# Attention values as the loaded operand in column halves, and softmax inverses applied afterwards to x

## The chip, the cores and the metric

The kernel runs on one core of a Trainium2 chip. The metric is the device time of one launch in microseconds; three runs of the kernel before gave 2671.84, 2673.00 and 2675.21 us, median 2673.0. The core has a matrix engine (TensorE, PE in the profile; its weight loads are a row of their own, PEld), VectorE (DVE), ScalarE (ACT), GpSimdE (POOL) and SyncE (SP), which here only issues DMAs. Each engine runs its own instructions in order and waits on semaphores that the others count up.

## The reference

Two layers of a hybrid block on 1024 tokens with 1024 features, fp32. Cut to the attention, which is what the change touches:

```
h = rms_norm(x); proj = h @ w_in             # q|k|v of mixer A, q|k|v of mixer B, two gates
A (8 heads of 64): per 64-token chunk, keys of the own chunk and 8 chunks before
   sc = q k^T / 8 + bias(relative distance);  p = softmax(sc);  y_a = (p v) @ w_branch_a
B (8 query heads, 2 key heads): rotary q, k; keys of 2 chunks
   m = max(max(sc), sink);  p = exp(sc - m) / (sum exp(sc - m) + exp(sink - m))
   y_b = (p v) @ w_branch_b
x = x + (sigmoid(gate_a) * y_a + sigmoid(gate_b) * y_b) @ w_out
x = x + SwiGLU(rms_norm(x));  after the last layer: rms_norm(x)
```

## The kernel before, in words

Activations lie feature-major (128 partitions are features, the free dimension is tokens). Most matmuls split fp32 numbers into a high and a low part (three matmuls each, `three` at L1191 to L1196 and `product` at L1203 to L1205). The attention of a layer is a hand-written pipeline over 128 units. Four groups g of 32 units follow each other; the first 16 units of a group are mixer A, the last 16 mixer B. A unit is one head and one block of queries: u is even for the first head of a pair (e = 0) and odd for the second (e = 1), and two neighbouring units share the block p. An A unit has 128 queries and nb = min(p + 1, 5) blocks of 128 keys, a B unit 2 times 64 queries (rows of both) and one block of 128 keys. So over the eight p of a group nb is 1, 2, 3, 4, 5, 5, 5, 5.

Every engine has its own loop `for s in range(UNITS + ...)`, and step s of each does the part that has come so far:
- PE: `scores(s)` (L1337, L1338), one gate step (three matmuls of 512 columns, L1191 to L1196), `turn(s - 2)` (L1348: transposes of the probabilities into PSUM tile `t_ps`), `weigh(s - 3)` (L1373), more gate steps, and each second step `turn_pair` (L1383). Gate steps are the fill: the tables `FILL_A` and `FILL_B` say how many stand in which step. Now and then `turn_values` (L1312) transposes two blocks of values.
- DVE: `row_max(s)` (L2603) adds the bias and takes the maximum of the scores; `invert_pair` (L2622) takes the reciprocals of two units; `take_heads` (L2632) multiplies the output of a pair by them on the way out of PSUM into `o_tok`. It also splits staged queries and keys and applies the rotary factors.
- ACT: `soften(s)` (L1741, the exponential with its row sum), `take_turned(s - 2)` (L1753, copies the turned probabilities from PSUM to `probs_t`), `take_pair` (L1764, L1767, copies the turned pair into `x_sb`), and copies of staged queries, keys and values.
- SP issues loads and stores: staged blocks, weight tiles, gate logits.

What the change starts from, in three lines: the turned probabilities are the loaded operand (128 columns) and 64 columns of values stream; the result has tokens on its partitions, so a pair of heads is scaled there and turned back by PE.

```
mm = pe.matmul(o_ps(u)[:, e * HD:(e + 1) * HD], probs_t[u % 2][:, j * P:(j + 1) * P], values[j], ...)   # L1373
dve.tensor_tensor(o_tok ..., o_ps(u) ..., inverse, ALU.mult)                                            # L2632
pe.transpose(p_ps, o_tok[:, n % 2, :], ident[:, :])                                                     # L1383
```

`t_ps`, the score tile of mixer A and the output tile of A are single: a turn waits until ACT has copied the one before it, scores of A until DVE has taken the maximum of the ones before. After the loop PE does `last_gates` (16 gate steps), ACT and DVE split `x_sb` into `o_hi` and `o_lo` (`split_o`, L1799, L2672), and `branches` uses these eight tiles in order.

## Time and profile before

| what | us |
|---|---|
| median of three runs | 2673.0 |
| profiled execution, whole | 2678.14 |
| its span, first to last instruction | 2676.2 |
| PE busy (share of the span) | 2631.9 (98%) |
| PEld, DVE, ACT busy | 2208.2 (83%), 1923.2 (72%), 1159.0 (43%) |

The span is cut by the program into two layers, and each layer into the input projection, the attention, the branches and output projection, and the feed-forward part. The profile has no names for these; they are found by the lines of the instructions. A matmul in fp32 (not split by hand) shows as two PE records, with a weight load each; a matmul of the split parts and a transpose show as one. In the timeline a record's length includes the way through the array, so neighbouring records overlap: what one costs in a full stream is the distance from its start to the next start.

### The profile page before, as it was taken

How to read it: one execution, taken by the hardware profiler on the slowest of the kernel's cores; microseconds unless marked ns; L12 is line 12 of the kernel's file. 1: busy time of each engine (PE TensorE's matmuls, PEld its weight loads, DVE VectorE, ACT ScalarE, POOL GpSimd, SP SyncE). 2: the span in 40 equal slices, each digit the busy share in tenths (PEclk: the TensorE clock that was granted, in tenths of full speed). 3: DMA queues.
4: the chain of work that ended last, by engine and by line, in shares of the span. 5: the costliest groups of instructions: out<-in, count | busy, mean ns of one | idle time of the engine just before them, and what ended most of it. 6: DMA issues, size and time to landing. Idle time of an engine off the chain costs nothing. (4 is left out here: it accounts for less than half of the span.)

```text
span 2676.2 us, 36725 instructions
## 1 busy us (share of the span) xinstructions
PE 2631.9 (98%) x12920; PEld 2208.2 (83%) x12920; DVE 1923.2 (72%) x3579; ACT 1159.0 (43%) x2429; POOL 252.6 (9%) x390
## 2 busy tenths in 40 slices
PE   8999999999999999999999999999999999999998
PEld 6888888888888888888878888888888888888886
DVE  8766667644787787767996666775448887776687
ACT  6222677732533333344542227775325333333444
POOL 0000311244100000000000011112440000000000
PEclk9999999999999999999999999999999999999999
DMA  4323433253222332385423243332531332234843
GB/s 147 122 104 115 155 102 111 75 183 115 87 99 103 114 118 84 106 269 176 153 99 122 99 144 123 119 97 88 188 120 61 114 110 88 103 114 136 267 124 126
DMA packets 185236, 333.21 MB, mean 125 GB/s; under 512 B 17248, under 2 KB 62688, under 8 KB 185056
## 3 DMA queue, kind: packets, MB, share of 16 engines
q1 hardware_dynamic: 176832, 307.67, 34.6%
q10 hardware_dynamic: 8224, 23.20, 2.6%
q8 instruction: 105, 1.72, 0.3%
q14 instruction: 75, 0.61, 0.1%
HBM read 237.09 MB, written 92.80 MB: 123 GB/s over the span
## 5 line engine op out<-in xcount | busy, mean ns | idle before, releaser
L1203 PE MATMUL ps<-op_hi,up_hi 128*128 128x512 f32 x1232 | 479.9, 390 | 2.5 <-DVE third_sum L2781 2.5
L1205 PE MATMUL ps<-op_hi,up_lo 128*128 128x512 f32 x1232 | 479.3, 389 | 0.0
L1204 PE MATMUL ps<-op_lo,up_hi 128*128 128x512 f32 x1232 | 479.3, 389 | 0.0
L1203 PE MATMUL ps<-in_hi,up_hi 128*128 128x512 f32 x728 | 286.9, 394 | 3.3 <-DVE up_lo L2279 2.1
L1205 PE MATMUL ps<-in_hi,up_lo 128*128 128x512 f32 x728 | 285.0, 392 | 0.0
L1204 PE MATMUL ps<-in_lo,up_hi 128*128 128x512 f32 x728 | 285.0, 392 | 0.0
L1878 ACT ACTIVATE up_hi<-up_raw 128x512 fp32r<-128x512 f32 x252 | 158.0, 630 | 276.9 <-PE ps L1205 271.1
L1203 PEld LDWEIGHTS ps<-op_hi,up_hi 128*128 128x128 f32 x1232 | 231.3, 188 | 51.1 <-issue 3.3
L1205 PEld LDWEIGHTS ps<-op_hi,up_lo 128*128 128x128 f32 x1232 | 231.3, 188 | 48.3
L1204 PEld LDWEIGHTS ps<-op_lo,up_hi 128*128 128x128 f32 x1232 | 231.3, 188 | 47.6
L1173 POOL CAST w_hi<-w_raw 128x256 fp32r<-128x256 f32 x192 | 85.3, 486 | 1757.7 <-DMA w_raw<-w_lin 1199.7
L1203 PE MATMUL ps<-act_hi,dn_hi 128*128 128x512 f32 x616 | 240.5, 390 | 1.4 <-DVE dn_lo L2956 1.4
L1204 PE MATMUL ps<-act_lo,dn_hi 128*128 128x512 f32 x616 | 239.7, 389 | 0.0
L1205 PE MATMUL ps<-act_hi,dn_lo 128*128 128x512 f32 x616 | 239.7, 389 | 0.0
L1592 ACT ACTIVATE up_hi<-w_quarter 128x512 fp32r<-128x512 f32 x156 | 96.7, 628 | 192.5 <-PE ps L1205 180.4
L1905 ACT ACTIVATE act_hi<-act_raw 128x512 fp32r<-128x512 f32 x154 | 97.0, 630 | 176.1 <-DMA act_raw<-ff_saved 173.3
L2748 DVE TENSOR_TENSOR up_lo<-up_raw,up_hi 128x512 fp32r<-128x512 f32 x252 | 172.7, 687 | 0.0
L1177 POOL TENSOR_TENSOR w_lo<-w_raw,w_hi 128x256 fp32r<-128x256 f32 x192 | 168.6, 907 | 0.0
L1203 PEld LDWEIGHTS ps<-in_hi,up_hi 128*128 128x128 f32 x728 | 138.1, 190 | 33.0 <-DVE up_lo L2279 4.1
L2954 DVE TENSOR_TENSOR act_lo<-act_raw,act_hi 128x512 fp32r<-128x512 f32 x154 | 106.3, 690 | 82.0 <-ACT act_hi L1905 81.3
L1204 PEld LDWEIGHTS ps<-in_lo,up_hi 128*128 128x128 f32 x728 | 138.1, 190 | 28.5
L1205 PEld LDWEIGHTS ps<-in_hi,up_lo 128*128 128x128 f32 x728 | 137.7, 189 | 28.9
(266 smaller groups left out, 5406.8 us busy)
## 6 DMA issues: line engine op xcount, KB each, us to landing
up_raw<-w_gu SPq DMA_DIRECT2D x42, 1024.0 KB, 5.1
act_raw<-ff_saved SPq DMA_DIRECT2D x154, 256.0 KB, 2.7
w_quarter<-w_lin SPq DMA_DIRECT2D x52, 512.0 KB, 4.4
w_raw<-w_lin SPq DMA_DIRECT2D x48, 512.0 KB, 3.7
ff_saved<-ff_block SPq DMA_DIRECT2D x88, 256.0 KB, 2.0
ff_saved<-ff_mix SPq DMA_DIRECT2D x66, 256.0 KB, 2.1
gated<-gates_saved SPq DMA_DIRECT2D x32, 512.0 KB, 4.1
stage<-in_saved SPq DMA_DIRECT2D x48, 256.0 KB, 2.8
```

The costliest lines, as they stand in the source:

```text
L1173: pool.tensor_copy(w_hi[slot][:, k, :], w_raw[raw][:, k, :]).then_inc(hi_made, 1)
L1177: op = pool.tensor_tensor(w_lo[slot][:, k, :], w_raw[raw][:, k, :], w_hi[slot][:, k, :], ALU.subtract)
L1203: pe.matmul(out, w1, x1, start=first, stop=False, skip_group_check=True)
L1204: pe.matmul(out, w1, x0, start=False, stop=False, skip_group_check=True)
L1205: return pe.matmul(out, w0, x1, start=False, stop=last, skip_group_check=True)
L1592: act.activation(up_hi[s % PRODUCTS][:, :, :], in_weight(q, i), ACT.Copy).then_inc(in_raised, 1)
L1878: act.activation(up_hi[s % PRODUCTS][:, :, :], up_src(q, i), ACT.Copy).then_inc(up_raised, 1)
L1905: act.activation(act_hi[r][:, :], act_raw[r][:, :], ACT.Copy).then_inc(act_raised, 1)
L2748: dve.tensor_tensor(up_lo[s % PRODUCTS][:, :, :], up_src(q, i), up_hi[s % PRODUCTS][:, :, :], ALU.subtract).then_inc(up_split, 1)
L2954: dve.tensor_tensor(act_lo[r][:, :], act_raw[r][:, :], act_hi[r][:, :], ALU.subtract)
```

## The change

The operands of `weigh` change places: 64 columns of values are loaded and the 128 turned probabilities stream. The two heads of a pair write partitions 0 to 63 and 64 to 127 of the output, so that each uses half of the array's columns, and the two heads alternate. The result is feature-major and goes unscaled into `x_sb` (DVE copies it from PSUM). `turn_pair`, `o_tok` and `take_pair` go. The reciprocals are taken for eight units at a time, turned by PE as an 8 by 128 block (`turn_inverse`, step 8k + 10 for units 8k to 8k + 7), copied to SBUF by DVE, stored to DRAM by SP (step 8k + 11), loaded back as rows that are repeated over 64 partitions each (steps 8k + 12 and 8k + 16, four units each time) and multiplied into `x_sb` in place by DVE (steps 8k + 15 and 8k + 19). There are three `probs_t` instead of two. In mixer B two units are turned one after the other and copied at once. `weigh` runs once per pair, at even steps. The gate steps keep their number per phase and move between steps (`FILL_A`, and `FILL_B`'s rounding); all logits but the last go through one buffer; `vb_odd` lies in two pieces.

```diff
 NPROBS = 3
-NSTAT = 8
+NTURNED = 3
+ODD_FIRST = 3
+NSTAT = 16
...
-FILL_A = ((3, 3, 3, 2, 2, 2, 2, 1, 1, 1, 1, 1, 1, 1, 1, 1), (1, 1, 1, 1, 1, 0, 1, 0, 1, 0, 0, 0, 1, 0, 0, 0))
+FILL_A = ((3, 3, 3, 3, 2, 3, 1, 2, 1, 1, 0, 1, 1, 1, 0, 1), (1, 1, 0, 1, 0, 1, 0, 1, 0, 1, 0, 1, 0, 1, 0, 0))
...
+TURNED_AT, SAVED_AT, SPREAD_AT, SCALED_AT = 10, 11, (12, 16), (15, 19)
...
-        probs_t = [at(f"probs_t{i}", [P, A_COLS], F32, 101 * KB + 2560 * i) for i in range(2)]
+        probs_t = [at(f"probs_t{i}", [P, A_COLS], F32, (101 * KB, 103 * KB + 512, TAB + 5 * KB + 512)[i]) for i in range(NTURNED)]
...
+        inverse_rows = at("inverse_rows", [P, 2 * P], F32, TAB + 14592)
...
+            def save_inverse(L, eight):
+
+                n = L * EIGHTS + eight
+                sp.wait_ge(inverse_step, 2 * n + 2)
+                sp.dma_start(inverse_dram[n], inverse_turned[0:EIGHT, :]).then_inc(inverse_saved, 16)
+
+            def spread_inverse(L, quarter):
+
+                n = L * QUARTERS + quarter
+                sp.wait_ge(inverse_saved, 16 * (n // 2 + 1))
+                if n > 0:
+                    sp.wait_ge(head_scaled, n)
+                for e in range(2):
+                    src = inverse_dram[n // 2][QUARTER * (n % 2):QUARTER * (n % 2 + 1), :].rearrange("(p e) n -> e p n", e=2)
+                    sp.dma_start(inverse_rows[e * HD:(e + 1) * HD, :].rearrange("d (p n) -> d p n", p=2),
+                                 src[e:e + 1].to_broadcast([HD, 2, P])).then_inc(inverse_spread, 16)
...
-                for s in range(UNITS + 3):
+                for s in range(UNITS + SPREAD_AT[1]):
+                    if eight_at(s, SAVED_AT) is not None:
+                        save_inverse(L, eight_at(s, SAVED_AT))
+                    for quarter in quarters_at(s, SPREAD_AT):
+                        spread_inverse(L, quarter)
...
-                    pe.wait_ge(turned_ready, L * UNITS + u)
+                if u > 0 and (mixer == "A" or e == 0):
+                    pe.wait_ge(turned_ready, L * TURN_GROUPS + groups_turned(u - 1))
...
+                first = e if mixer == "B" else 0
                 for j in range(key_blocks(mixer, p)):
-                    mm = pe.transpose(t_ps[:, j * P:(j + 1) * P], probs[u % NPROBS][:, j * P:(j + 1) * P], ident[:, :])
+                    mm = pe.transpose(t_ps[:, (first + j) * P:(first + j + 1) * P], soft(u)[:, j * P:(j + 1) * P], ident[:, :])
                 mm.then_inc(turned, 1)
...
             def weigh(L, u):
 
...
                 nb = key_blocks(mixer, p)
+                n = L * HEAD_PAIRS + u // 2
                 if mixer == "A":
...
+                    blocks = [va[:, p + 1 - nb + j, :] for j in range(nb)]
+                    turns = [turned_to(u - 1), turned_to(u)]
...
                 else:
...
+                    blocks = [vb[:, chunk // 2, :] if chunk % 2 or chunk == 0 else odd_values(chunk // 2 - 1)]
+                    turns = [turned_to(u)[:, e * P:(e + 1) * P] for e in range(2)]
...
-                pe.wait_ge(turned_ready, L * UNITS + u + 1)
-                n = L * (UNITS // 2) + u // 2
...
+                pe.wait_ge(turned_ready, L * TURN_GROUPS + groups_turned(u))
                 taken = n - 1 if mixer == "B" and u % PHASE > 1 else n
-                if e == 0 and taken > 0:
+                if taken > 0:
                     pe.wait_ge(head_free, taken)
                 for j in range(nb):
-                    mm = pe.matmul(o_ps(u)[:, e * HD:(e + 1) * HD], probs_t[u % 2][:, j * P:(j + 1) * P], values[j],
-                                   start=(j == 0), stop=(j == nb - 1))
+                    for e in range(2):
+                        rows = slice(e * HD, (e + 1) * HD)
+                        mm = pe.matmul(o_ps(u)[rows, :], blocks[j][:, rows], turns[e][:, j * P:(j + 1) * P],
+                                       start=(j == 0), stop=(j == nb - 1))
                 mm.then_inc(head_done, 1)
 
-            def turn_pair(L, u):
-
-                n = L * (UNITS // 2) + u // 2
-                pe.wait_ge(head_free, n + 1)
-                if n > 0:
-                    pe.wait_ge(pair_ready, n)
-                pe.transpose(p_ps, o_tok[:, n % 2, :], ident[:, :]).then_inc(pair_turned, 1)
+            def turn_inverse(L, s, eight):
+
+                pe.wait_ge(inverse_step, 2 * (L * EIGHTS + eight) + 1)
+                if values_before(s) > 0:
...
+                pe.transpose(i_ps, inverse[:, stats_of(eight)], ident[:, :]).then_inc(inverse_turned_done, 1)
...
-                for s in range(UNITS + 5):
+                for s in range(UNITS + 3):
+                    steps = fill_steps(s)
+                    if s % PHASE == 0 and s > 0:
+                        for i, k in steps[:1]:
+                            gate_step(L, i, k)
+                        steps = steps[1:]
                     if s < UNITS:
                         scores(L, s)
-                    steps = fill_steps(s)
                     for i, k in steps[:1]:
                         gate_step(L, i, k)
-                    if 2 <= s < UNITS + 2:
-                        turn(L, s - 2)
-                    if 3 <= s < UNITS + 3:
+                    u = s - 2
+                    if 0 <= u < UNITS:
+                        if unit(u)[0] == "A":
+                            turn(L, u)
+                        elif u % 2:
+                            turn(L, u - 1)
+                            turn(L, u)
+                    if eight_at(s, TURNED_AT) is not None:
+                        turn_inverse(L, s, eight_at(s, TURNED_AT))
+                    if s >= 4 and s % 2 == 0:
                         weigh(L, s - 3)
                     for i, k in steps[1:]:
                         gate_step(L, i, k)
-                    if s > 5 and s % 2 == 0:
-                        if values_before(s) > 0:
-                            pe.wait_ge(v_ready, L * VALUES + values_before(s))
-                        turn_pair(L, s - 5)
                     for c, part in turns_at(s):
-                        if s > 6:
-                            pe.wait_ge(pair_ready, L * (UNITS // 2) + (s - 5) // 2)
+                        if inverses_before(s + 1) > 0:
+                            pe.wait_ge(inverse_step, 2 * (L * EIGHTS + inverses_before(s + 1)))
                         turn_values(L, c, part)
...
-                act.activation(probs_t[u % 2][:, 0:cols], t_ps[:, 0:cols], ACT.Copy).then_inc(turned_ready, 1)
...
+                act.activation(turned_to(u)[:, 0:cols], t_ps[:, 0:cols], ACT.Copy).then_inc(turned_ready, 1)
...
             def split_o(L):
-                act.wait_ge(pair_ready, (L + 1) * (UNITS // 2))
+                act.wait_ge(head_free, (L + 1) * HEAD_PAIRS)
+                act.wait_ge(inverse_saved, 16 * (L + 1) * EIGHTS)
                 for j in range(KT):
+                    if j == 0:
+                        act.wait_ge(head_scaled, (L + 1) * QUARTERS - PHASE // QUARTER)
+                    if j == KT - 2:
+                        act.wait_ge(head_scaled, (L + 1) * QUARTERS)
                     if j == XK:
...
+            def take_inverse(L, eight):
+
+                n = L * EIGHTS + eight
+                dve.wait_ge(inverse_turned_done, n + 1)
+                if n > 0:
+                    dve.wait_ge(inverse_saved, 16 * n)
+                dve.tensor_copy(inverse_turned[0:EIGHT, :], i_ps).then_inc(inverse_step, 1)
 
             def take_heads(L, u):
 
-                n = L * (UNITS // 2) + u // 2
-                dve.wait_ge(head_done, L * UNITS + u + 1)
-                dve.wait_ge(inverse_ready, n + 1)
-                if u >= 4:
-                    dve.wait_ge(pair_turned, n - 1)
-                inverse = stat[:, u % NSTAT - 1:u % NSTAT + 1, 6:7].to_broadcast([P, 2, HD])
-                dve.tensor_tensor(o_tok[:, n % 2, :].rearrange("p (e d) -> p e d", e=2),
-                                  o_ps(u).rearrange("p (e d) -> p e d", e=2), inverse, ALU.mult).then_inc(head_free, 1)
...
+                n = L * HEAD_PAIRS + u // 2
...
+                dve.wait_ge(head_done, n + 1)
+                src = o_ps(u) if mixer == "A" else o_ps(u).rearrange("p (h n) -> p h n", h=2)
+                dve.tensor_copy(x_of(u), src).then_inc(head_free, 1)
...
+            def scale_heads(L, quarter):
+
+                mixer, g, _, p = unit(QUARTER * quarter)
+                n = L * QUARTERS + quarter
+                dve.wait_ge(head_free, L * HEAD_PAIRS + 2 * quarter + 2)
+                dve.wait_ge(inverse_spread, 32 * (n + 1))
+                if mixer == "A":
+                    x = x_sb[:, g, p * P:(p + 2) * P]
+                    dve.tensor_tensor(x, x, inverse_rows[:, :], ALU.mult).then_inc(head_scaled, 1)
...
-                for s in range(UNITS + 5):
+                for s in range(UNITS + SCALED_AT[1]):
+                    if s < UNITS:
+                        row_max(L, s)
+                    if eight_at(s, TURNED_AT) is not None:
+                        take_inverse(L, eight_at(s, TURNED_AT))
                     if s % 2 == 1 and 5 <= s < UNITS + 4:
                         take_heads(L, s - 4)
-                    if s < UNITS:
-                        row_max(L, s)
-                    if s % 2 == 0 and 1 <= s <= UNITS:
-                        invert_pair(L, s - 1)
+                    for late in range(2):
+                        eight = eight_at(s - late, EIGHT)
+                        if eight is not None:
+                            sunken = unit(EIGHT * eight)[0] == "B"
+                            if late == 0 and sunken:
+                                add_sinks(L, eight)
+                            if late == (1 if sunken else 0):
+                                invert(L, eight)
+                    for quarter in quarters_at(s, SCALED_AT):
+                        scale_heads(L, quarter)
```

Below, L numbers in the rows of the changed kernel are its own: L1440 and L1441 are the scores (L1337 and L1338 before), L1452 the turn (L1348), L1480 `weigh` (L1373), L1489 `turn_inverse`, L1294 to L1299 a gate step (L1191 to L1196), L1415 `turn_values` (L1312).

On PE, first layer, group 0 of mixer A, at the units with two key blocks, the rows before are:

```order
L1348 MATMUL ps<-ident,probs_107 128x128 x3
L1373 MATMUL ps<-va,probs_t_110 128x64 x2
L1191 MATMUL ps<-in_hi_52,w_hi_225 128x512
L1195 MATMUL ps<-in_lo_59,w_hi_225 128x512
L1196 MATMUL ps<-in_hi_52,w_lo_227 128x512
L1383 MATMUL ps<-ident,o_tok 128x128
L1337 MATMUL ps<-ka_hi_92,qs_88 128x512
L1338 MATMUL ps<-ka_lo_94,qs_88 128x512
L1191 MATMUL ps<-in_hi_52,w_hi_225 128x512
L1195 MATMUL ps<-in_lo_59,w_hi_225 128x512
L1196 MATMUL ps<-in_hi_52,w_lo_227 128x512
L1348 MATMUL ps<-ident,probs_108 128x128 x3
```

and with the change, from the same turn on:

```order
L1452 MATMUL ps<-ident,probs_108 128x128 x3
L1480 MATMUL ps<-probs_t_112,va 64x128
L1480 MATMUL ps<-probs_t_110,va 64x128
L1480 MATMUL ps<-probs_t_112,va 64x128
L1480 MATMUL ps<-probs_t_110,va 64x128
L1440 MATMUL ps<-ka_hi_92,qs_88 128x512
L1441 MATMUL ps<-ka_lo_94,qs_88 128x512
L1294 MATMUL ps<-in_hi_52,w_hi_231 128x512
L1298 MATMUL ps<-in_lo_59,w_hi_231 128x512
L1299 MATMUL ps<-in_hi_52,w_lo_233 128x512
L1452 MATMUL ps<-ident,probs_109 128x128 x3
```

The output matmuls of a unit (two rows of one kind before) have become four, alternating between the two heads, all in one step of the pair; the next step has none, and the pair's transpose is gone.

On PE, same group, between two turns of full length (five key blocks), the rows before are:

```order
L1348 MATMUL ps<-ident,probs_106 128x128 x5
L1373 MATMUL ps<-va,probs_t_109 128x64 x5
L1312 MATMUL ps<-ident,stage_103 128x128 x2
L1337 MATMUL ps<-ka_hi_91,qs_87 128x256
L1338 MATMUL ps<-ka_lo_93,qs_87 128x256
L1337 MATMUL ps<-ka_hi_91,qs_87 128x384
L1338 MATMUL ps<-ka_lo_93,qs_87 128x384
L1191 MATMUL ps<-in_hi_50,w_hi_225 128x512
L1195 MATMUL ps<-in_lo_57,w_hi_225 128x512
L1196 MATMUL ps<-in_hi_50,w_lo_227 128x512
L1348 MATMUL ps<-ident,probs_107 128x128 x5
```

and with the change:

```order
L1452 MATMUL ps<-ident,probs_109 128x128 x5
L1415 MATMUL ps<-ident,stage_103 128x128 x2
L1440 MATMUL ps<-ka_hi_91,qs_87 128x256
L1441 MATMUL ps<-ka_lo_93,qs_87 128x256
L1440 MATMUL ps<-ka_hi_91,qs_87 128x384
L1441 MATMUL ps<-ka_lo_93,qs_87 128x384
L1452 MATMUL ps<-ident,probs_107 128x128 x5
L1480 MATMUL ps<-probs_t_111,va 64x128
```

Between these two turns stood the output matmuls of a unit, values, scores and a gate step; now values and scores stand there, and the output matmuls of both units come behind the second turn.

On DVE, first layer, in a phase of mixer B, the rows before are (`o_tok` is the scaled pair):

```order
L2603 ISA probs_106,stat<-ps,b_zeros,less_sinks 128x128
L2603 ISA stat 128x1
L2620 TENSOR_TENSOR stat<-stat 128x2
L2622 RECIPROCAL stat<-stat 128x2
L2551 TENSOR_TENSOR ka_lo_94<-stage_102,ka_hi_92 128x512
L2632 TENSOR_TENSOR o_tok<-ps,stat 128x128
L2603 ISA probs_107,stat<-ps,b_zeros,less_sinks 128x128
L2603 ISA stat 128x1
L2609 TENSOR_TENSOR stat<-sink_rows,stat 128x2
```

and with the change (`inverse_turned` are the turned reciprocals, `inverse_rows` what came back from DRAM):

```order
L2736 TENSOR_TENSOR sink_term<-row_sum,sink_term 128x8
L2738 RECIPROCAL inverse<-sink_term 128x8
L2715 ISA probs_109,neg_max<-ps,b_zeros,less_sinks 128x128
L2715 ISA neg_max 128x1
L2746 COPY inverse_turned<-ps 8x128
L2715 ISA probs_107,neg_max<-ps,b_zeros,less_sinks 128x128
L2715 ISA neg_max 128x1
L2758 COPY x_sb<-ps 128x2x64
L2768 TENSOR_TENSOR x_sb<-x_sb,inverse_rows 128x256
L2715 ISA probs_108,neg_max<-ps,b_zeros,less_sinks 128x128
L2715 ISA neg_max 128x1
```

The multiplication out of PSUM and the two small instructions of each pair are gone; a plain copy, the turned reciprocals and a multiplication in `x_sb` stand there, and the maximum of the next scores (L2715, L2603 before) is queued behind each of them.

## Rows read from the trace of the kernel before

**Rows 1.** The page, part 1: busy time of each engine.

```profile
PE 2631.9 (98%) x12920; PEld 2208.2 (83%) x12920; DVE 1923.2 (72%) x3579; ACT 1159.0 (43%) x2429; POOL 252.6 (9%) x390
```

**Rows 2.** Stretches: the attention of both layers (busy us, granted clock, DMA).

```profile
282.00:530.00 248.00, 240.29 (x1684) 213.98 (x1684) 166.63 (x551) 183.00 (x563) 43.64 (x63) 0.99 0.34 105
1592.00:1840.00 248.00, 241.29 (x1700) 215.64 (x1698) 168.01 (x559) 179.59 (x560) 36.03 (x59) 1.00 0.34 106
```

**Rows 3.** Groups by line on PE, 281 to 533 us: records, busy, mean ns.

```profile
L1373 PE MATMUL ps<-va,probs_t 128*128 128x64 f32 x480 | 60.9, 269 | 1.0 <-DVE o_tok L2632 1.0
...
L1373 PE MATMUL ps<-vb,probs_t 128*128 128x64 f32 x72 | 12.2, 251 | 0.1
...
L1373 PE MATMUL ps<-vb_odd,probs_t 128*128 128x64 f32 x56 | 9.3, 248 | 0.0
```

**Rows 4.** Timeline of PE, mixer A, five key blocks (start us, length us).

```profile
1807.16 1.23 PE L1373 MATMUL ps<-va,probs_t 128*128 128x64 f32 x10
...
1808.26 0.36 PE L1337 MATMUL ps<-ka_hi,qs 128*128 128x256 f32 x1
...
1808.93 0.71 PE L1348 MATMUL ps<-ident,probs 128*128 128x128 f32 x5
1809.48 1.23 PE L1373 MATMUL ps<-va,probs_t 128*128 128x64 f32 x10
...
1811.73 1.23 PE L1373 MATMUL ps<-va,probs_t 128*128 128x64 f32 x10
```

**Rows 5.** Timeline of PE: fp32 records with one streamed column, and with 128.

```profile
2032.29 1.84 PE L1214 MATMUL ps<-ones,sumsq 128*128 128x1 f32 x16
2033.99 0.49 PE L1203 MATMUL ps<-op_hi,up_hi 128*128 128x512 f32 x1
...
2050.45 1.95 PE L1235 MATMUL ps<-ident,rstd_col 128*128 128x128 f32 x16
2052.15 0.48 PE L1203 MATMUL ps<-op_hi,up_hi 128*128 128x512 f32 x1
```

**Rows 6.** Timeline, PE's rows, one unit of mixer B.

```profile
392.39 0.27 PE L1348 MATMUL ps<-ident,probs 128*128 128x128 f32 x1
...
392.95 0.45 PE L1191 MATMUL ps<-in_hi,w_hi 128*128 128x512 f32 x1
...
393.25 0.40 PE L1195 MATMUL ps<-in_lo,w_hi 128*128 128x512 f32 x1
...
393.71 0.27 PE L1348 MATMUL ps<-ident,probs 128*128 128x128 f32 x1
```

**Rows 7.** Groups by line and shape on ACT, 281 to 533 us.

```profile
L1741 ACT ACTIVATE probs<-probs,stat 128x640 f32<-128x640 f32 x32 | 26.4, 826 | 0.4
L1741 ACT ACTIVATION_READ_ACCUMULATOR probs<-probs,stat 128x1 f32 x128 | 24.4, 190 | 0.0
L1753 ACT ACTIVATE probs_t<-ps 128x640 f32<-128x640 f32 x32 | 22.5, 703 | 17.3 <-PE ps L1348 16.7
```

**Rows 8.** Timeline: from a turn through ACT's copy to the next turn.

```profile
1836.78 0.27 PE L1348 MATMUL ps<-ident,probs 128*128 128x128 f32 x1
...
1837.09 0.28 ACT L1753 ACTIVATE probs_t<-ps 128x128 f32<-128x128 f32 x1 [0.49 <-PE ps L1348]
...
1837.51 0.30 PE L1348 MATMUL ps<-ident,probs 128*128 128x128 f32 x1 [0.29 <-ACT probs_t L1753]
```

**Rows 9.** DMA issues, 281 to 533 us: count, KB each, us to landing.

```profile
gates_saved<-logit SPq DMA_DIRECT2D x14, 256.0 KB, 2.1
...
swapped<-in_saved SPq DMA_DIRECT2D x28, 64.0 KB, 2.4
```

**Rows 10.** Timeline, end of the second layer's attention: DVE, and PE's first branch matmul.

```profile
1841.70 5.93 DVE L2672 TENSOR_TENSOR o_lo<-x_sb,o_hi 128x1024 fp32r<-128x1024 f32 x4 [2.00 <-ACT o_hi L1799]
1848.62 4.81 DVE L2672 TENSOR_TENSOR o_lo<-x_sb,o_hi 128x1024 fp32r<-128x1024 f32 x4 [0.98 <-ACT o_hi L1799]
```

**Rows 11.** Timeline of PE, the same place.

```profile
1852.76 0.39 PE L1191 MATMUL ps<-o_hi,w_hi 128*128 128x512 f32 x1
```

More of the change, by code:

```diff
@@ L45 @@
 NPROBS = 3
-NSTAT = 8
+NTURNED = 3
+ODD_FIRST = 3
+NSTAT = 16
+QUARTER = 4
 GROUPS = 4
@@ L264, in unit, with number_b, eight_at, quarters_at @@
     return "AB"[r // PHASE], g, r % 2, r % PHASE // 2
-def number_b(u):
-    g, r = divmod(u, UNITS_PER_GROUP)
-    return g * PHASE + r - PHASE + 1
+def number_b(eight):
+    g, r = divmod(EIGHT * eight, UNITS_PER_GROUP)
+    return (g * PHASE + r - PHASE) // EIGHT
+def eight_at(s, at):
+    return (s - at) // EIGHT if s >= at and (s - at) % EIGHT == 0 and s - at < UNITS else None
+def quarters_at(s, at):
+    return [2 * eight_at(s, a) + j for j, a in enumerate(at) if eight_at(s, a) is not None]
+def own_steps(L, sinks):
+    return L * (1 + 2 * B_EIGHTS) + 1 + sinks
+def inverses_before(s):
+    return sum(eight_at(j, TURNED_AT) is not None for j in range(s))
+def groups_turned(u):
+    g, r = divmod(u + 1, UNITS_PER_GROUP)
+    return g * (PHASE + PHASE // 2) + min(r, PHASE) + max(r - PHASE, 0) // 2
+TURN_GROUPS = GROUPS * (PHASE + PHASE // 2)
+HEAD_PAIRS = UNITS // 2
+QUARTERS = UNITS // QUARTER
+EIGHT = 2 * QUARTER
+EIGHTS = UNITS // EIGHT
+B_EIGHTS = EIGHTS // 2
+TURNED_AT, SAVED_AT, SPREAD_AT, SCALED_AT = 10, 11, (12, 16), (15, 19)
 def raw_slot(t):
@@ L557, in o_ps, with x_of, stat_of, stats_of @@
             return bank(5 if mixer == "B" and u // 2 % 2 else 6)[:, 0:P]
+        def x_of(u):
+            mixer, g, _, p = unit(u)
+            if mixer == "A":
+                return x_sb[:, g, p * P:(p + 1) * P]
+            tile, chunk = GROUPS + g // 2 * 2, chunk_of(g, p)
+            return x_sb[:, tile:tile + 2, chunk * CHUNK:(chunk + 1) * CHUNK]
+        def stat_of(u):
+            return slice(u % NSTAT, u % NSTAT + 1)
+        def stats_of(eight):
+            first = EIGHT * eight % NSTAT
+            return slice(first, first + EIGHT)
+        i_ps = bank(7)[0:EIGHT, 2 * P:3 * P]
+        def turned_to(u):
+            mixer, _, _, _ = unit(u)
+            return probs_t[u % NTURNED if mixer == "A" else u // 2 % 2]
+        def odd_values(block):
+            return vb_odd[0][:, block, :] if block < ODD_FIRST else vb_odd[1][:, block - ODD_FIRST, :]
+        def logit_of(i):
+            return logit[1 if i == GATE_HALVES - 1 else 0][:, :]
+        def soft(u):
+            mixer, _, _, _ = unit(u)
+            first = u // NPROBS % 2 * P if mixer == "B" else 0
+            return probs[u % NPROBS][:, first:first + (P if mixer == "B" else A_COLS)]
+        def soft_last(u):
+            mixer, _, _, _ = unit(u)
+            return u - (2 * NPROBS if mixer == "B" and u % PHASE >= NPROBS else NPROBS)
         v_ps = bank(7)[:, 0:2 * P]
@@ L1738, in soften @@
                 act.wait_ge(scores_free, L * UNITS + u + 2)
[L1739 to L1745 removed]
+                buf = soft(u)
@@ L1782, in attention @@
                         soften(L, s)
+                    if eight_at(s, EIGHT) is not None and unit(s - 1)[0] == "B":
+                        soften_sinks(L, eight_at(s, EIGHT))
                     for e in range(2):
```

168 lines of the change are left out of this document (89 added, 79 removed).

## The prediction

> **What bounds the kernel now.** I read the busy times first, then the stretches of the two attentions, PE's groups by line there, and the timeline of single units. The reader is to see that PE is busy for 98% of the span [rows 1], and for 240 and 241 of the 248 us of each attention at a granted clock of 0.99 to 1.00, its upper level of 2.4 GHz, while ACT is busy for 183 and DVE for 168 us at most [rows 2]. So a us that PE loses in the attention is a us of the kernel, as long as the others can follow. The change touches nothing outside the two attentions and their ends.
>
> What PE's time consists of there: sixteen fp32 records that stream one column each take 1.70 us (2032.29 to 2033.99), and sixteen that stream 128 columns take 1.70 us as well (2050.45 to 2052.15), 0.106 us a record [rows 5]. A record of 64 columns cannot be cheaper, then: what it pays for is the load of 128 columns, not its stream. The output matmuls have 480, 72 and 56 such records in the first layer, 608 [rows 3], so 608 x 0.106 = 64.4 us per layer. The unit of five key blocks shows the whole: 2.32 us from one unit's output matmuls to the next with a pair transpose between, 2.25 without, scores 0.67 (1808.26 to 1808.93), turn 0.55 [rows 4].
>
> **The change part by part, per layer.**
>
> Output matmuls. The same number of matmuls and records is left (two heads times nb blocks times two records for each pair), but each loads 64 columns, streams 128, and the two heads use different halves of the array. I take a record's stream at 0.106, which [rows 5] give as its most, and let the halves overlap: the second record of one head runs beside the first of the other, so a pair takes 2nb + 1 slots of 0.106 instead of 4nb. Mixer A: nb adds up to 30 over eight pairs, 68 slots, times four groups 272; mixer B: 32 pairs of 3 slots, 96. 368 x 0.106 = 39.0 us: a gain of 25.4. If the halves do not overlap it is 608 slots again and the gain is 0; no record of before uses half of the array, so these are the ends.
>
> The Trainium skill ("TensorE: Matmul & The Clock Gate", LDWEIGHTS) says that a weight load costs its columns at 1.2 GHz, whatever the rows; by it 64 columns cost an estimated 53 ns. The one-column rows agree with it at 128 columns (0.106 against its 0.107); no row here loads 64.
>
> Pair transposes. 64 go, at 0.07 each (2.32 less 2.25): 4.5 gained. 16 transposes of reciprocals come, at most the same: 1.1 lost.
>
> Switches between the whole array and its halves. Before, every matmul has the whole array; now PE goes to halves and back for each of 64 pairs, and once more for each of 16 reciprocal blocks: 144 switches per layer. No trace shows one. From below: 0. From above: the next load waits until the record before has left the array, 0.269 mean length [rows 3] less 0.106 = 0.163, and then stands open for 0.106: 0.27. The nearest thing that the trace shows is a load that is not covered: the first 512-column record behind short ones takes 0.30 (392.95 to 393.25) where the next two take 0.23 each (393.25 to 393.71) [rows 6]. I take this 0.07, since a switch at the least uncovers a load: 144 x 0.07 = 10.1 lost.
>
> New wait for the copy. `t_ps` is single. Before, between two turns lay output matmuls and scores; now, from an odd step to the next even one, only scores, and sometimes values or a gate step. The way through ACT: 0.31 from a record's start to the copy's start (1836.78 to 1837.09), 0.14 from the copy's end to the next turn [rows 8], and a copy of 640 columns takes 0.703 [rows 7]. Five records of a turn: 0.44 + 0.31 + 0.70 + 0.14 = 1.59 from its start, against 0.55 + 0.67 = 1.22 without the wait: 0.37. A gate step (three times 0.23) covers it wholly, a pair of values mostly. Behind the first group this leaves, for each group, two units at 0.37, one of four blocks at about 0.26 and some 0.6 for the small ones: 1.6, times three 4.8; the first group has gate steps there. 4.8 lost. Queued behind the waiting turn on PE are the output matmuls of a pair and the next scores, so DVE and ACT wait with it.
>
> Reciprocals through DRAM. DVE wants the rows five steps after it has copied the turned block, then four steps after that. A small store lands after 2.1 and a small load after 2.4 us [rows 9]: 4.5, with handoffs about 5, against five units of mixer B at 1.32 (392.39 to 393.71, [rows 6]), 6.6. It fits, so I put it at 0; behind a late row DVE's next maximum would be queued, and PE's scores behind that. SP stands still for these landings too, and stage loads queue behind it; 2 us of that lie within the steps that these loads are ahead.
>
> End of the attention. The last four pairs' rows need the store and two loads one behind the other, 6.9 us, before `split_o` may take the last tiles; on DVE the whole of `o_lo` stands behind that multiplication. Before, `o_lo` runs from 1841.70 to 1853.43 [rows 10] and PE wants the eight tiles from 1852.76 on [rows 11], one per 0.69 (three records of 0.23, [rows 6]), the last at 1857.6. About 6 us later (the pair's transpose and copies drop out of the way) `o_lo` would end at 1859.4, 1.8 late: 1.8 lost.
>
> DVE and ACT. DVE's maximum and ACT's exponential stay; 64 multiplications out of PSUM become copies, 64 pairs of reciprocals become 16 blocks, 32 multiplications of 256 columns come; ACT loses the pair copies and half of B's turn copies. Both get lighter and have room [rows 2]: 0. The gate steps keep their number: 0. The logit store lands within 2.1 us [rows 9], the next logit is three units away at the nearest: 0.
>
> Sum per layer: -25.4 - 4.5 + 1.1 + 10.1 + 4.8 + 1.8 = -12.1; two layers -24.2. The profiled execution took 2678.1, so 2653.9; it lies 5.1 over the median of the runs, so 2648.8, told as 2649.
>
> **The rivals.**
>
> Drained switches (slower). Each switch waits for the array to empty. For it: a record's length of 0.269 is 0.163 longer than its slot [rows 3], and mixed modes are new here. Against it: nothing shows that the wait is needed. At 0.20 a switch costs 28.8 per layer instead of 10.1: +6.6, in all +13.2, 2686. It decides from 0.154 on, where 144 switches eat up the rest of the sum (22.2). The Trainium skill ("TensorEngine Tiling", Key Properties) says that changing the tiling mode drains TensorE, which speaks for this rival, and that tiles run in parallel, which speaks for the overlap; no run shows either so far.
>
> Halves one behind the other (slower). The two heads follow each other, or the loads stay at 0.106 each, so 4nb slots stay. For it: no overlap of two matmuls is in this trace. Against it: they touch different array columns and PSUM partitions. The gain of 25.4 goes: +13.3 per layer, 2700.
>
> The chain of DVE and ACT becomes the bound (about the same). ACT spends 0.826 + 0.190 + 0.703 = 1.72 on a unit of five blocks [rows 7], DVE's maximum stands between scores and scores. PE would come down to (1.34 + 1.10 + 11 x 0.106 + 0.14) / 2 = 1.87 without gate steps. If such a unit stops at 2.15, the 32 of a layer give back 9 us: 2667. Against it: both engines lose work.
>
> Late reciprocals (about the same or slower). If DVE waits 1 us for each of 32 quarters and PE gets half of it, 16 us per layer: 2681. For it: the margin in mixer B is 1.6 us only.
>
> **How the numbers follow.** Forecast 0.50: 2649, its own range 2634 to 2663 (switches at 0.02 to 0.12). Drained switches 0.20 around 2686 (up to 2706 at 0.27). Serial halves 0.11 at 2700. Chain 0.12 at 2667. Late rows 0.07 at 2681. With switches that cost nothing the sum is 2629. A measurement of this kernel can tell 0.2%, 5.3 us, from no change: 2667.7 to 2678.3. Faster: 0.50, 0.09 of the chain and 0.03 of the last, 0.62; same 0.09 (the rest of the chain, 0.02 of the late rows, 0.04 of the drained); slower 0.29. The range that holds 8 in 10 goes from 2627 to 2692: it reaches over the drained switches and leaves out most of the serial halves and the full drain.
>
> **What would show it.** Right: two records of different halves that start together or 0.106 apart and a pair of five blocks in about 1.2 us; attentions shorter by some 12 us each; waits of a turn for ACT's copy of about 0.4 at even steps; no wait of DVE for `inverse_rows`. Wrong: a gap of over 0.15 before the first output matmul and behind the last one (drained), ten blocks in 2.1 us (serial), DVE waiting for DMA rows, or PE waiting for scores to be taken in units of five blocks.

## The result, and the profile after

The changed kernel takes 2683.1 us (median, 2679.7 to 2687.0) against 2673.0 for the kernel before on the same chip: a ratio of 1.0035, 95% interval 1.0024 to 1.0046. It is slower by 10 us where 24 us faster was forecast. The profiled execution has a span of 2683.3 us.

The output matmuls became about as cheap as forecast. The stretches of both attentions in the changed kernel, to be set beside [rows 2] (us, busy time of PE, of its weight loads, of DVE, ACT and POOL, granted clock, DMA share and GB/s):

```profile
282.00:530.00 248.00, 230.07 (x1644) 175.00 (x1642) 158.81 (x495) 165.46 (x442) 35.15 (x60) 0.99 0.39 116
1592.00:1840.00 248.00, 230.12 (x1632) 175.76 (x1631) 162.03 (x495) 159.85 (x432) 35.90 (x59) 0.99 0.40 121
```

PE, DVE and ACT are all less busy than before, PE by 10 and 11 us, and yet the attentions are no shorter: what PE saved it now waits. From the first maximum on DVE to the last it is 235.0 and 237.8 us, where before it was 234.1 and 232.7. PE's idle time from the first scores of an attention to its last output matmul, added up over the trace, is 17.9 and 19.5 us, where before it was 7.1 and 6.2.

A pair of units with five key blocks on PE in the changed kernel (start, length, line, what ended the idle time before), to be set beside [rows 4]:

```profile
1812.33 0.74 PE L1452 MATMUL ps<-ident,probs 128*128 128x128 f32 x5 [0.21 <-ACT probs_t L1877]
1813.00 1.31 PE L1480 MATMUL ps<-probs_t,va 128*64 128x128 f32 x20
1814.24 0.39 PE L1440 MATMUL ps<-ka_hi,qs 128*128 128x256 f32 x1
...
1815.62 0.71 PE L1452 MATMUL ps<-ident,probs 128*128 128x128 f32 x5
...
1816.68 0.33 PE L1441 MATMUL ps<-ka_lo,qs 128*128 128x384 f32 x1
1817.21 0.30 PE L1452 MATMUL ps<-ident,probs 128*128 128x128 f32 x1 [0.20 <-ACT probs_t L1877]
```

The 20 records of both heads take 1.24 us (1813.00 to 1814.24; the first row of the next kind tells the end). The pair repeats after 4.88 us (1812.33 to 1817.21), the wait for ACT's copy in it, against 5.26 before with a gate step (2.32, 2.25 and 0.69 for the gate).

Where PE waits now is seen at 391 to 403 us, in mixer B of the second group. SP's queue, ACT, PE, and the granted clock (last but two column) there:

```profile
390.27 1.26 SPq L1150 DMA_DIRECT2D inverse_rows<-inverses_saved  x2
391.63 1.79 SPq L1017 DMA_DIRECT2D stage<-in_saved  x2
```

```profile
396.26 0.63 ACT L1809 ACTIVATE ka_hi<-stage 128x512 fp32r<-128x512 f32 x1 [2.29 <-DMA stage<-in_saved]
396.80 0.36 ACT L1877 ACTIVATE probs_t<-ps 128x256 f32<-128x256 f32 x1
```

```profile
395.16 0.40 PE L1299 MATMUL ps<-in_hi,w_lo 128*128 128x512 f32 x1
397.22 0.44 PE L1480 MATMUL ps<-probs_t,vb_odd 128*64 128x128 f32 x4 [1.66 <-ACT probs_t L1877]
...
398.52 0.63 PE L1298 MATMUL ps<-in_lo,w_hi 128*128 128x512 f32 x1
```

```profile
393.00:397.00 4.00, 2.56 (x16) 1.00 0.49 135
397.00:400.00 3.00, 2.78 (x12) 0.62 0.47 129
400.00:403.00 3.00, 3.00 (x18) 0.81 0.24 89
```

Read it as a chain. SP issues the stage load of the keys (391.63, with 0.7 us of waiting for DVE's `ka_lo` in it) only behind the two loads of a quarter's reciprocals, which belong to the same step. ACT stands 2.29 us for that load; the copy of the turned probabilities, next in ACT's queue, comes late; PE's output matmuls wait 1.66 us for it, and behind that pause the granted clock is 0.62 over 3 us, near its lower level of 1.2 GHz (a gate record takes 0.63 instead of 0.40). In the first attention PE's output matmuls wait for ACT's copy six times, the wait above among them (us in total, times, longest):

```profile
PE ps L1480 <- ACT probs_t L1877: 5.8, 6, 1.7
```

What SP itself waits for in the first attention:

```profile
SPq L1147 <- DVE x_sb L2768: 30.7, 16, 8.5
SPq L1140 <- DVE inverse_turned L2746: 22.9, 12, 4.3
SPq L1147 <- DVE x_sb L2772: 19.2, 10, 3.5
```

The next load of rows stands behind DVE's multiplication by the rows before (both rows of `x_sb`), 50 us in all, and all else on SP stands behind it. ACT's wait for `stage` in `ka_hi` in the two attentions, first in the kernel before, then in the changed one:

```profile
ACT ka_hi L1696 <- DMA stage<-in_saved: 2.0, 2, 1.6
ACT ka_hi L1696 <- DMA stage<-in_saved: 4.4, 2, 4.1
```

```profile
ACT ka_hi L1809 <- DMA stage<-in_saved: 5.8, 4, 2.3
ACT ka_hi L1809 <- DMA stage<-in_saved: 13.0, 7, 4.1
```

The wait of 4.1 us in the second attention is there in both.

The end of the first attention, on DVE and PE, to be set beside [rows 10, 11]:

```profile
519.87 0.56 DVE L2772 TENSOR_TENSOR x_sb<-x_sb,inverse_rows 128x256 f32<-128x256 f32 x1 [1.03 <-DMA inverse_rows<-inverses_saved]
523.84 0.43 DVE L2772 TENSOR_TENSOR x_sb<-x_sb,inverse_rows 128x256 f32<-128x256 f32 x1 [3.41 <-DMA inverse_rows<-inverses_saved]
527.67 0.42 DVE L2772 TENSOR_TENSOR x_sb<-x_sb,inverse_rows 128x256 f32<-128x256 f32 x1 [3.40 <-DMA inverse_rows<-inverses_saved]
528.02 9.17 DVE L2825 TENSOR_TENSOR o_lo<-x_sb,o_hi 128x1024 fp32r<-128x1024 f32 x8
```

```profile
529.45 0.40 PE L1294 MATMUL ps<-o_hi,w_hi 128*128 128x512 f32 x1
...
531.56 0.50 PE L1294 MATMUL ps<-o_hi,w_hi 128*128 128x512 f32 x1 [0.17 <-DVE o_lo L2825]
...
532.70 0.50 PE L1294 MATMUL ps<-o_hi,w_hi 128*128 128x512 f32 x1 [0.17 <-DVE o_lo L2825]
```

Three legs of load and multiplication follow one another, and all of `o_lo` stands behind them. PE starts a branch tile every 1.14 us, DVE's pace, instead of every 0.69.

### The profile page after: what moved, and what is told of

It is laid out like the page before. It is cut to its first block and busy times, and to the rows that moved or that the text cites. A ratio compares the mean times of both kernels' runs of the same rounds, so it can differ in the third digit from the quotient of the medians.

```text
span 2683.3 us, 36122 instructions
## 1 busy us (share of the span) xinstructions
PE 2614.9 (97%) x12824; PEld 2128.1 (79%) x12824; DVE 1916.7 (71%) x3483; ACT 1124.6 (42%) x2189; POOL 245.9 (9%) x390
## 5 line engine op out<-in xcount | busy, mean ns | idle before, releaser
L1280 POOL TENSOR_TENSOR w_lo<-w_raw,w_hi 128x256 fp32r<-128x256 f32 x192 | 161.2, 869 | 0.0
```

The lines of the kernel that those rows point to most:

```text
L1280: op = pool.tensor_tensor(w_lo[slot][:, k, :], w_raw[raw][:, k, :], w_hi[slot][:, k, :], ALU.subtract)
```

## Experiments

All start from the changed kernel unless a diff says otherwise; the kernel before ran beside them with medians of 2671.5 to 2673.5. Each ratio is to that. The differences in us are those of the medians. The intervals of the ratios are about 0.001 wide to each side, so a difference between two changed kernels is uncertain by some 4 us; where a reading is finer than that, it rests on the traces or is not shown.

**SP's order.**

```diff
-  save_inverse / spread_inverse    # first in SP's step
   load_rope, shift_values, load_half(L, c)
+  save_inverse / spread_inverse    # behind the stage loads
```

> Only SP's order is changed: within a step, the store and the two loads of the reciprocals are issued behind the stage loads of that step instead of ahead of them. Theory Q (SP's queue: the stage loads of the keys stand behind the reciprocals' DMAs and their waits, so ACT's `ka_hi` is late, ACT's copy of the turned probabilities behind it is late, and PE waits and loses its upper clock): ACT's wait for `stage` falls from 5.8 and 9.0 us per attention to about 2, PE's output matmuls wait 2 to 4 us less per attention, time 2675 to 2679. Theory C (a chain of PE, ACT and DVE is too tight whatever SP does): within 2 us of the changed kernel, 2681 to 2685. Theory M (matmuls and switches are dearer than thought): no change.

2678.7 us, ratio 1.0020 (1.0011 to 1.0029): 4.4 less. ACT's wait for `stage` in `ka_hi` fell to 2.4 and 6.0 us. At the place shown above the keys' load now comes first, ACT waits 0.30 us for it instead of 2.29, and PE's wait of 1.66 us is gone:

```profile
389.94 1.09 SPq L1017 DMA_DIRECT2D stage<-in_saved  x2
391.13 1.25 SPq L1150 DMA_DIRECT2D inverse_rows<-inverses_saved  x2
```

```profile
393.27 0.63 ACT L1809 ACTIVATE ka_hi<-stage 128x512 fp32r<-128x512 f32 x1 [0.30 <-DMA stage<-in_saved]
```

```profile
PE ps L1480 <- ACT probs_t L1877: 2.3, 3, 1.4
PE ps L1440 <- DVE neg_max L2715: 5.2, 8, 1.6
```

The last two rows are PE's waits in the first attention: those for ACT's copy fell from 5.8, while those for DVE's maximum rose from 3.0. Theory Q holds, for a part.

**The whole way of the reciprocals left out.**

```diff
-  turn_inverse, take_inverse, save_inverse, spread_inverse, scale_heads
```

> The whole way of the reciprocals is left out: no transposes of reciprocals, no copy of them, no DRAM, no multiplication in `x_sb`; the output stays without its normalisation. Theory R (the way of the reciprocals costs what the matmuls gain: PE's 16 transposes with their waits, SP's queue, DVE's work and the tail of the attention, some 3.3 us of `o_lo` per layer): 2683 less 2 x (about 3 for the transposes and their waits, 3 to 4 for late stage loads, 3 to 5 for the tail) = 2659 to 2667. Theory C (chain of PE, ACT and DVE): only the transposes and the tail go, 2 x (2 + 3) = 10, about 2673. Theory M: 2 x 2 for transposes and switches, about 2679.

2651.8 us, ratio 0.9923 (0.9910 to 0.9935): 31 less than the changed kernel, more than any theory gave, and 21 less than the kernel before. So two thirds of the gain that the forecast had without this way (32) are there, and the way takes them back with 10 us more.

**Halves one behind the other.**

```diff
-  for j in range(nb):
-      for e in range(2):
+  for e in range(2):
+      for j in range(nb):
```

> The output matmuls of a pair are issued head after head instead of alternating, everything else as in the changed kernel: it measures what the alternation of the halves gives. If two neighbouring records overlap only when they use different halves: a five-block pair takes about 2.1 us instead of 1.24, the attention loses 25 us per layer less what waits absorb (up to 10): 2715 to 2733. If a record with 64 columns is cheap by itself, whatever its neighbour: no change, 2683. The theories on waits say nothing here; theory M would want the overlap to be worth less than the 25 us per layer of the forecast.

2708.6 us, ratio 1.0131 (1.0117 to 1.0145): 25 more. The pair of five blocks on PE:

```profile
434.76 2.02 PE L1480 MATMUL ps<-probs_t,va 128*64 128x128 f32 x20
436.71 0.39 PE L1440 MATMUL ps<-ka_hi,qs 128*128 128x256 f32 x1
```

1.95 us instead of 1.24. Records of one half follow each other 0.109 apart, although they load 64 columns only; records of different halves start 0.006 apart. The alternation is the gain. The loss is smaller than expected because the last records of the first head still run beside the first ones of the second.

**Gate steps on even steps.**

```diff
-FILL_A = ((3,3,3,3,2,3,1,2,1,1,0,1,1,1,0,1), (1,1,0,1,0,1,0,1,0,1,0,1,0,1,0,0))
+FILL_A = ((3,3,3,3,2,3,1,2,1,1,1,0,1,1,1,0), (1,1,1,0,1,0,1,0,1,0,1,0,1,0,0,0))
```

> The table of gate steps is changed so that in mixer A a gate step lies in the even steps, between the two turns that have only scores between them, instead of in the odd ones (second row 1110101010101000, first row with its two zeros at 11 and 15); the sums stay. Theory C (the wait for ACT's copy): the 0.2 to 0.4 us waits of the turn go, about 6 to 8 of them per attention, and DVE's maxima get more time: 2 to 4 us per layer, 2676 to 2680. Theory Q: these waits only hide others, within 2 us of 2683.

2690.9 us, ratio 1.0072 (1.0060 to 1.0085): 8 more, against both theories. PE's waits for DVE's maximum before scores in the first attention, first in the changed kernel, then here:

```profile
PE ps L1440 <- DVE neg_max L2715: 3.0, 8, 0.7
```

```profile
PE ps L1440 <- DVE neg_max L2715: 10.3, 21, 0.7
```

An odd step without a gate has only a turn between two scores, and by these rows that is too short for DVE's maximum. The gate step covers either this wait or the smaller one for ACT's copy.

**Loads and multiplication left out.**

```diff
-  spread_inverse(L, quarter)      # SP
-  scale_heads(L, quarter)         # VectorE
```

> Left out: the two loads of each quarter's rows and the multiplication in `x_sb` that uses them (so the output stays without its normalisation). Kept: the transposes of the reciprocals with their waits, the copy on VectorE, the store to DRAM. Without the whole way the kernel took 2651.8, with it 2683: 31 us to divide. Theory Q+T (SP's queue and the tail: the loads, their waits for `x_sb` and the late end of the attention carry most): 2657 to 2664. Theory P (PE's transposes and their waits carry most, 16 per layer and one 1.6 us wait): 2670 to 2678.

2660.3 us, ratio 0.9952 (0.9941 to 0.9964): 23 of the 31 us go. Theory Q+T holds; 8.5 are left for transposes, copies and stores.

**Transposes of reciprocals later in their step.**

```diff
-  turn_inverse(...)    # before weigh
   weigh, gate steps
+  turn_inverse(...)    # and take_inverse last in VectorE's step
```

> The transpose of eight reciprocals moves behind the output matmuls and gate steps of its step, and VectorE takes it at the end of its step instead of right behind the maximum. Theory P: the wait of that transpose for ACT's copy of the values (1.63 us once per attention) and for VectorE's reciprocals (0.3 to 1.0) goes, and VectorE no longer waits 5 us per attention for it: 2 to 3 us per layer, 2677 to 2680. Theory Q+T: these waits are only moved, 2681 to 2685.

2676.9 us, ratio 1.0016 (1.0007 to 1.0025): 6 less, at the edge of theory P's range. One wait that shrank, to 0.60, stood in the changed kernel as

```profile
307.84 0.27 PE L1489 MATMUL ps<-ident,inverse 128*8 128x128 f32 x1 [1.63 <-ACT va L1844]
```

since the turned reciprocals lie in the PSUM bank that ACT reads the values from, and the program lets PE wait for that. DVE's wait for the turned reciprocals, which theory P named too, did not go: 6.1 us in the first attention, 5.5 in the changed kernel. So it is not shown that the waits which theory P named are what gave back the 6 us.

**The end of the attention.**

```diff
+  last_rows = two tiles in the stage buffers, for the last two quarters (loaded without head_scaled)
-  scale_heads of the last three quarters in the loop
+  scale_heads of the last three quarters in split_o, before o_lo[6]
```

> End of the attention: the rows of the last two quarters have a place of their own and are loaded at once, without waiting for the multiplication before, and VectorE subtracts the first six `o_lo` tiles before it waits for the last three quarters. Theory T (the tail): one leg of 3.4 us goes and `o_lo` is no longer behind the rows, so PE's first branch tiles come 0.69 apart instead of 1.14: 3 to 4 us per layer, 2675 to 2677. If the tail hides behind something else that is late (the gate logits, POOL's weights): 2681 to 2684.

2676.9 us, ratio 1.0012 (1.0003 to 1.0021): 6 less, theory T.

**The three together.** Diff: those of the first experiment and the last two.

> The three rearrangements together: rows behind the stage loads on SP (alone 2678.7), transposes of reciprocals later in their step, and the tail with places of its own. If the parts add up: 4 + 5 + 7 = 16 less than 2683, 2667, and so below the kernel before (2673). If they hide each other: 2673 to 2677.

2665.0 us, ratio 0.9968 (0.9956 to 0.9980): they add up, 18 less than the changed kernel, and it is faster than the kernel before. On DVE the end of the first attention is now

```profile
515.89 8.02 DVE L2838 TENSOR_TENSOR o_lo<-x_sb,o_hi 128x1024 fp32r<-128x1024 f32 x6 [2.52 <-ACT o_hi L1921]
523.83 0.41 DVE L2782 TENSOR_TENSOR x_sb<-x_sb,inverse_rows 128x256 f32<-128x256 f32 x1
524.17 0.75 DVE L2782 TENSOR_TENSOR x_sb<-x_sb,last_rows 128x256 f32<-128x256 f32 x2
```

with no idle time for the rows, and ACT's wait in the second attention, 13.0 in the changed kernel, is

```profile
ACT ka_hi L1818 <- DMA stage<-in_saved: 6.5, 3, 3.9
```

**Loads kept, multiplication left out.**

```diff
-  sp.wait_ge(head_scaled, n)
+  sp.wait_ge(inverse_spread, 32 * n)
-  scale_heads(L, quarter)
```

> The way of the reciprocals is kept up to the rows in SBUF, loads included; only VectorE's multiplication in `x_sb` is left out, and nothing waits for it any more (SP orders its loads by the landing of those before; the output stays without its normalisation). Without loads and multiplication the kernel took 2660.3, with both 2683. Theory Q (SP's queue: the loads by themselves hold up the stage loads): 2670 to 2676. Theory S (the multiplication: DVE's time, SP's wait for it before each next load, and the tail behind it): 2660 to 2664.

2666.4 us, ratio 0.9980 (0.9971 to 0.9989), between the two ranges, so neither theory holds alone: the loads cost 6 by themselves, the multiplication with what hangs on it 17.

**Multiplication on GpSimd**, in the kernel with the three rearrangements.

```diff
-  dve.tensor_tensor(x, x, rows, ALU.mult)
+  pool.tensor_tensor(x, x, rows, ALU.mult)    # between the weight tiles
```

> The three rearrangements (2665.0 together), and the multiplication of `x_sb` by the rows moves from VectorE to GpSimd, in its own order between the weight tiles; the result is the same. Theory S (DVE's 32 multiplications of 0.42 us, its waits for late rows of 4.4 us per attention, and SP's wait for the multiplication): 3 to 7 us less than 2665, 2658 to 2662. If the rest of the way (PE's transposes, the loads on SP) is what remains: 2663 to 2667. If GpSimd and VectorE disturb each other at their common work in SBUF: slower than 2667.

2662.0 us, ratio 0.9964 (0.9951 to 0.9976): 0.36% under the kernel before. The three alone have a ratio of 0.9968, and the intervals overlap almost wholly, so a gain over them is not shown and the theories are not told apart. GpSimd stands 78.0 and 45.3 us for rows in the first attention, which holds up none of DVE's maxima.

**Transposes later, without loads and multiplication.** Diff: those of the fifth and sixth experiments.

> As the kernel without loads and multiplication (2660.3), with the transpose of the reciprocals moved behind the output matmuls of its step and VectorE taking it at the end of its step. The whole way left out gave 2651.8. If the 8.5 us of transposes, copies and stores are waits (1.8 us for ACT's values and VectorE's reciprocals, VectorE standing 5 us per attention): 2654 to 2657. If they are work (16 transposes of 0.2 with their switches, 16 copies of 0.28): 2658 to 2661.

2654.2 us, ratio 0.9934 (0.9921 to 0.9946): by the medians 6 of the 8.5 us were waits and 2.5 are left for the work; the 2.5 are within the noise.

**Multiplication by a row that lies there.**

```diff
-  dve.wait_ge(inverse_spread, 32 * (n + 1));  x * inverse_rows
+  x * rstd[:, 0:256]        # SP as in the kernel with loads and no multiplication
```

> As the kernel with loads but without multiplication (2666.4), with the 32 multiplications of 128x256 back on VectorE at their places, but by a row that lies in SBUF anyway (`rstd`), so that they wait for no load and SP does not wait for them (the output has the wrong scale). With the true rows the kernel took 2683: 17 us for VectorE's time, SP's wait for the multiplication and the late rows with the tail behind them. If VectorE's time counts (32 x 0.42 = 13 us per layer on an engine that is 68% busy, some of it in front of a maximum): 2671 to 2677. If it is hidden and SP's wait and the tail carry it: 2665 to 2669.

2671.4 us, ratio 0.9995 (0.9986 to 1.0004): 5 for VectorE's time, which is hardly clear of the noise; so 11.7 of the 17 are waits behind late rows, of SP for the multiplication and of the tail for the rows.

**Short copies**, without the way of the reciprocals.

```diff
+  cols = P if mixer == "A" and u >= UNITS_PER_GROUP else cols
   act.activation(turned_to(u)[:, 0:cols], t_ps[:, 0:cols], ACT.Copy)
```

> As the kernel without the way of the reciprocals (2651.8), with ACT's copy of a unit's turned probabilities in mixer A, groups 1 to 3, cut to its first 128 columns (0.28 us instead of up to 0.70; the rest of the buffer keeps old values, so the output is wrong). Theory C (PE's waits for ACT's copy, forecast at 4.8 us per layer): 2642 to 2647. If VectorE's maximum is what ends last there: 2649 to 2652.

2647.7 us, ratio 0.9901 (0.9886 to 0.9917): 4.1 less by the medians, 6 by the ratios, between the two ranges. ACT's copy costs some 2 to 3 us per layer in these groups, against the forecast's 4.8. The traces agree that the forecast was too large: without the way of the reciprocals the turn waits six times per attention for the copy,

```profile
PE ps L1448 <- ACT probs_t L1869: 1.3, 6, 0.2
```

and with short copies 0.08 us are left of it.

## Why the prediction was wrong, point by point

**The failed step is "Reciprocals through DRAM ... so I put it at 0", with "DVE and ACT ... 0" and the tail.** Transposes with their switches and tail were forecast at 8 us in two layers; the way costs 31.3. The experiments divide it, by the medians: 6.1 for the loads on SP, 5.0 for VectorE's multiplications, 11.7 for waits behind late rows, 6.0 for waits around the transposes, 2.5 for their work. By the ratios it is 7.5, 4.0, 10.7, 4.8 and 2.9. Each is uncertain by some 4 us, so that only the loads and the waits behind late rows stand well clear of nothing, and another order of leaving things out could divide it differently. The forecast held a leg of 4.5 us, with handoffs 5, against five steps of 6.6 and saw that it fits. As the sign of a late row it named DVE's wait, and that wait is indeed almost absent but for the tail. It saw that SP stands still and that stage loads queue behind it, but counted only the landings, and set 2 us "within the steps that these loads are ahead" against them. SP's wait for DVE's multiplication by the rows before, 50 us in the first attention and up to 8.5 us at once, is not in it, and neither is that key loads and row loads fall into the same steps. "Both get lighter and have room" left out that what PE saves it can lose again to DVE's maximum: that wait before scores is 3.0 us in the first attention with the way of the reciprocals and without it, where the kernel before has 0.3.

**The tail** was put at 1.8 per layer by a delay of 6 us. `o_lo` starts at 528.02 and PE's first branch matmul at 529.45, but then `o_lo` runs at 1.14 per tile on DVE with nothing done ahead. From PE's first branch matmul to its last it is 90.0 and 88.4 us, where it is 86.8 in the kernel before and in every run in which `o_lo` does not stand behind loaded rows: 4.8 lost in two layers, not far from the forecast's 3.6. The rearranged tail gave back 6 by the medians.

**Output matmuls: mechanism right, terms off against each other.** The halves overlap fully: pairs of 20, 16, 12, 8 and 4 records take 1.24, 1.02, 0.81, 0.59 and 0.37, 42.8 us in a layer, against a forecast of 39.0 plus 4.5 for the switches back. Within that, a pair needs 2nb slots of 0.109, not 2nb + 1, and 1.24 less ten slots leaves 0.15 for switching, not 0.07. The way in costs 0.09 more, from the start of the turn's last record to that of the first output records, less a slot of 0.109:

```profile
1812.79 0.27 PE L1452 MATMUL ps<-ident,probs 128*128 128x128 f32 x1
1813.00 0.33 PE L1480 MATMUL ps<-probs_t,va 128*64 128x128 f32 x2
```

So a pair's two switches cost 0.24 together, where 0.14 was forecast, and the slot that is not needed pays for it. The transposes of the reciprocals add no switch of their own: where nothing is waited for, they start 0.109 behind the turn's last record. What was oversized is the kernel before. Of it the timeline in mixer B shows, between the rows of [rows 6]:

```profile
392.49 0.33 PE L1373 MATMUL ps<-vb_odd,probs_t 128*128 128x64 f32 x2
392.66 0.28 PE L1383 MATMUL ps<-ident,o_tok 128*128 128x128 f32 x1
392.70 0.30 PE L1337 MATMUL ps<-kb_hi,qb_second 128*128 128x128 f32 x1
```

Two records 0.17, not 0.21, and the pair's transpose 0.04, not 0.07: mixer B had nothing to win. Over a layer the groups of output matmuls add up to some 61 us instead of 64.4, each group taken at the median of its size. That is a part of why the kernel without the reciprocals is 21 us faster and not the forecast's 32. Another part is PE's wait in it for DVE's maximum, and a granted clock of 0.99 and 0.98 from the first scores of an attention to its last output matmul, where the kernel before has 1.00 over the same stretches (282 to 519 and 1604 to 1839 us). The execution shown lies 4 us over the median of this kernel:

```profile
PE ps L1436 <- DVE neg_max L2702: 3.0, 7, 1.1
```

```profile
279.00:508.00 229.00, 217.44 (x1583) 165.80 (x1582) 142.20 (x447) 158.28 (x436) 32.84 (x55) 0.99 0.33 103
1590.00:1818.00 228.00, 217.40 (x1583) 165.75 (x1582) 142.06 (x448) 158.38 (x436) 31.93 (x53) 0.98 0.33 104
```

How the 11 us divide among these is not shown.

**New wait for the copy:** 0.37 forecast for a pair of five blocks, 0.38 measured (from 1816.83, which is 0.67 of scores behind their start at 1816.16, to 1817.21). Its sum was too large, 4.8 against 2 to 3.

**Rivals.** Halves one behind the other: refuted by the serial kernel, which is 25 us slower. Drained switches: at 0.24 for two, a switch costs 0.12 on average, more than the forecast's 0.07 but under the 0.154 from which that rival decides. Across a switch the starts lie 0.20 apart, where a record is 0.27 long. The Trainium skill ("TensorEngine Tiling (Array Packing)", Key Properties) says that a mode change drains the engine; the measured gaps agree with a loss at each switch, without showing what drains. The chain of DVE and ACT: present, as the gate table shows (8 us for moving the gate steps by one) and the waits for DVE's maximum, but these waits are the same 3.0 us without the way of the reciprocals, so it is not what the way costs. Late reciprocals, priced at 2681 with 7 in 100: the time was right by luck, for the way was another, SP and the tail instead of DVE in front of a maximum.

Open stays how the 11.7 us divide between SP and the tail exactly, since the rearrangements share waits; the 4.8 of the tail are read from one trace. Open stays too how much of a pause's cost is the lower clock that follows some of them.

## What to carry to other kernels

A detour through DRAM is not priced by its latency against the steps until it is used, but by the queue that issues it: list what is issued behind each of its waits, and put loads that others need soon ahead of them. A step that is moved to the end of a phase needs its own count of legs, each with load, wait and multiplication. When an engine gets less to do, ask what its next instruction will then wait for: PE was 10 us less busy in an attention and won nothing.

## What the runs showed of the hardware

Two fp32 matmuls that stream 128 columns and use different column halves of the array run beside each other fully (0.006 apart, pairs 0.109 apart), while two of the same half need 0.109 each, though they load 64 columns and not 128: the load record of the output matmuls shrank (136 ns against 192), the slot did not. Going from the whole array to its halves and back cost 0.24 us per visit. A pause of PE of 1.66 us was followed by a granted clock of 0.62 over 3 us, so that a wait can cost more than its length; the pause of 1.63 us at 307.84 was not followed by a lower clock.
